# Other steps for the value pages of the paged attention in a hybrid decoder layer

## What is computed

```python
k_past = cache_k[l, page_table].reshape(db, past, N_HEADS, HEAD_DIM)
v_past = cache_v[l, page_table].reshape(db, past, N_HEADS, HEAD_DIM)
...
s = einsum('bqhd,bkhd->bhqk', q, k) * HEAD_DIM ** -0.5 + c_q - c_k
p = softmax(s)
return einsum('bhqk,bkhd->bqhd', p, v)
```

## Time and profile before

| | us |
|---|---|
| median of three runs | 2797.38 |
| lowest and highest run | 2797.11, 2801.74 |
| profiled execution | 2798.29 |
| its span, first to last instruction | 2796.3 |
| TensorE busy in the span | 2617.2 |
| VectorE busy | 1425.7 |
| ScalarE busy | 735.1 |

### The profile page before, as it was taken

How to read it: one execution, slowest core, us unless ns; L and a number is a source line. 1 busy time by engine, 2 the same in 40 slices (tenths; PEclk the granted TensorE clock), 3 DMA queues, 4 the chain that set the end, 5 groups by cost and what they waited for, 6 DMA issues and landing times.

```text
span 2796.3 us, 50751 instructions
## 1 busy us (share of the span) xinstructions
PE 2617.2 (94%) x19729; PEld 2342.8 (84%) x19729; DVE 1425.7 (51%) x5631; ACT 735.1 (26%) x1029; POOL 160.9 (6%) x326
## 2 busy tenths in 40 slices
PE   6788789999988799889999999999999999999998
PEld 3676667777776356569999999999999999999998
DVE  5698768767867622244434343434343434343433
ACT  5222123333332311132222222222222222222221
POOL 0100111111111122100000000000000000000000
PEclk8888889999989799979999999999999999999999
DMA  8778999999999897652222222222222222222221
GB/s 297 242 243 299 335 334 364 360 359 359 335 328 363 323 314 265 218 186 84 93 96 91 91 91 91 91 91 91 91 91 91 91 91 91 91 91 91 91 91 65
DMA packets 272292, 524.55 MB, mean 188 GB/s; under 512 B 16148, under 2 KB 181693, under 8 KB 270740
## 3 DMA queue, kind: packets, MB, share of 16 engines
q1 hardware_dynamic: 218717, 365.71, 38.0%
q0 software_dynamic: 39760, 142.46, 13.8%
q10 hardware_dynamic: 13575, 13.14, 1.4%
HBM read 501.84 MB, written 17.76 MB: 186 GB/s over the span
## 4 chain that ended last, share of the span: by engine, by line
PE 70%; DMA 13%; DVE 11%; issue 3%; SPq 2%; ACT 1%; POOL 0%; DVEq 0%; POOLq 0%; ACTq 0%
PE ps L749 69%; DMA t_r<-in_cache_k 9%; DVE t_r L1857 8%; DMA t_r<-in_cache_v 2%; DMA t_wraw<-in_w_in 1%; SPq L630 1%; PE ps L752 1%; DVE t_stg L1742 0%; DVE t_wlr L1686 0%; DVE t_S L1857 0%; DVE t_auxL L1686 0%; DVE t_work L1686 0%; DVE t_xl L1686 0%; SPq L683 0%; ACT t_wh L1271 0%
## 5 line engine op out<-in xcount | busy, mean ns | idle before, releaser
L749 PE MATMUL ps<-t_xh,t_wh 128*128 128x260 f32 (+1 forms) x4352 | 1080.3, 299 | 33.4 <-DVE t_wlr L1686 19.6
L749 PE MATMUL ps<-t_xl,t_wh 128*128 128x260 f32 (+1 forms) x4352 | 1053.1, 294 | 0.0
L749 PEld LDWEIGHTS ps<-t_xh,t_wh 128*128 128x128 f32 x4352 | 745.8, 193 | 166.7 <-issue 119.2
L1686 DVE TENSOR_TENSOR t_wl<-t_wraw,t_wh 128x1024 fp32r<-128x1024 f32 x296 | 362.3, 1225 | 843.7 <-ACT t_wh L1271 843.7
L1271 ACT ACTIVATE t_wh<-t_wraw 128x1024 fp32r<-128x1024 f32 x376 | 398.5, 1060 | 1479.9 <-PE ps L749 1369.8
L749 PEld LDWEIGHTS ps<-t_xl,t_wh 128*128 128x128 f32 x4352 | 744.7, 193 | 10.7 <-issue 1.4
L749 PE MATMUL ps<-t_xh,t_wl 128*128 128x260 f32 (+1 forms) x3072 | 677.1, 294 | 0.0
L1857 DVE CUSTOM_DVE_ANT_0 t_r<-t_r,t_work 128x128 f32<-128x128 f32 x2048 | 455.4, 286 | 175.3 <-DMA t_r<-in_cache_k 159.0
L749 PEld LDWEIGHTS ps<-t_xh,t_wl 128*128 128x128 f32 x3072 | 487.5, 189 | 11.8
L749 PE MATMUL ps<-t_xh,t_wlr 128*128 128x260 f32 x1280 | 376.1, 294 | 0.0
L749 PE MATMUL ps<-t_hh,t_wh 128*128 128x260 f32 x1408 | 282.8, 282 | 3.4 <-issue 3.4
(11 more groups left out here) (305 smaller groups left out, 1243.0 us busy)
## 6 DMA issues: line engine op xcount, KB each, us to landing
t_r<-in_cache_k SPq DMA_DIRECT2D x256, 512.0 KB, 6.7
t_r<-in_cache_v POOLq DMA_DIRECT2D x256, 512.0 KB, 7.0
t_wraw<-in_w_up SPq DMA_DIRECT2D x44, 2048.0 KB, 8.0
t_wraw<-in_w_down SPq DMA_DIRECT2D x22, 2048.0 KB, 7.8
t_wraw<-in_w_in SPq DMA_DIRECT2D x21, 2048.0 KB, 16.2
t_wraw<-in_w_o SPq DMA_DIRECT2D x11, 2048.0 KB, 14.0
scr_x<-t_r POOLq DMA_DIRECT2D x1, 4160.0 KB, 20.0
t_work<-in_x_prompt SPq DMA_DIRECT2D x4, 1024.0 KB, 6.6
```

Source lines behind the costliest of these rows:

```text
L749: return pe.matmul(out, lhsT, rhs, start=start, stop=stop)
L1686: return dve.tensor_tensor(out, in0, in1, op)
```

## The change

One line of `page_slots` gives other rates for the value pages. During the input projection a step takes two pages, and four in every eighth step (7, 15, 23, ...) where it was every fourth. In steps 80 to 83 it takes two where it took four. From step 84 on every step takes four, where every third took two.

```diff
         while done < PAGES:
-            rate = (4 if at % 4 == 3 else 2) if at < CHUNKS else 4 if at < OUT0 or at % 3 else 2
+            rate = (4 if at % 8 == 7 else 2) if at < CHUNKS else 2 if at < OUT0 else 4
             take = min(rate, PAGES - done)
             values[at] = [r * PAGES + done + i for i in range(take)]
             done += take
```

## The result

The changed kernel takes 2805.6 us in the median, the kernel before 2799.3 on the same chips: 1.0022 of before, with an interval of 1.0013 to 1.0031. It is 6.4 us slower, where 2.1 us faster had been forecast. The profiled execution has a span of 2803.7 us, against 2796.3 before. One execution of 13982 us, of the run that thins both bytes and products, is left out of that run's median.

A forecast was written before the change was run, and what follows sets the result against it. Projection bound mostly by the loop of key page landing, VectorE scoring and buffer reload; output steps by TensorE. -14.8 - 2.5 - 4.5 + 11.9 + 1.8 + 6 = -2.1 us: 2796.2 against the profiled run, 2795.3 beside the median; range 2781 to 2809.

The forecast's parts named there:

- Output steps: Steps 86 to 110: 11.9 us more for pairs, 1.8 for an end of a sequence, 6 for stalls.
- The pairs: Output steps: 11 more pairs of value pages at 1.08 us of TensorE each, 11.9 us slower, nothing covering it.
- 18, so 6 more than now: Output steps: TensorE's stalls for value pages rise from 12.2 us to 18; bounds of the increase 0 and 20.
- Rival B: Output steps become bound by landings and lose 30 to 34 us; kernel 8 to 12 slower, 2807; chance 0.12.
- Projection: Steps 17 to 78: eight dropped pairs win 14.8 us (bounds 0 and 22.7), moved sequence ends 2.5; about 636 us.
- the price of a pair: Projection: a dropped pair wins 2.1 us where the chain runs over key pages and VectorE, 1.08 where over TensorE.
- The step-30 term: Projection: TensorE's 7.70 us wait before its first pair at step 30 goes, winning 2.5 us, between 0 and 7.7.
- the sign that the prediction had named against itself: Projection: TensorE's wait before a sequence's first pair, at step 30, reappears in another step with a like size.
- Middle: Steps 79 to 85: TensorE's waits for value pages go, VectorE is late next; 4.5 us won, bounds 0 and 5.5.
- Tail: Behind step 110: sample softmax one step later costs nothing, covered by TensorE's output chunks; without cover up to 6.9 us.
- A: Projection held by DMA alone: 22.7 us won there, -15.5 for the kernel, so 2782; chance 0.33.
- C: Projection doesn't follow DMA load; VectorE's 488 us and order set the pace; only some 5 us won, 2807; chance 0.14.

## Why the prediction was wrong, point by point

*Output steps: the step that failed.* The forecast's sum there was 19.7 us, and 30.5 came: 10.8 more, against 3.9 more than forecast that the stages ahead won, and 2.3 that came from the steps before 17, which no edit touches. The pairs were right: TensorE's count rises from 1089 matmuls to 1177, that is 11 pairs of eight; the fourth end of a sequence, priced at 1.8, falls into step 111, where nothing more than 0.3 us came. The mis-sized term is "18, so 6 more than now" for landings: the row that it was counted from went from 12.2 to 26.5 us, 14.3 more (inside the bound of 20). Of the 18.6 us beside the pairs, the six output weight loads make about 9 (the windows with small loads on either schedule), so this mechanism was near its size. The rest came from three places that the forecast had not priced: the stores and the feed-forward load (4.6 us in steps 93 and 110, shown by moving them); the residual rows in steps 87 and 89 (the chain's landings of 9.2 us; two pages in these steps won 3.5 us beside the moved pairs); and a granted clock of 0.98 in place of 1.00 over 242 us. It is short of full in three places, steps 87, 89 and 104:

```profile
948.79:964.06 15.27, 12.68 (x66) 7.64 (x62) 3.17 (x4) 2.65 (x5) 3.16 (x6) 0.89 1.01 364
971.95:986.12 14.17, 11.71 (x62) 6.47 (x58) 2.18 (x2) 2.64 (x3) 2.11 (x4) 0.88 0.70 253
1118.77:1128.11 9.34, 9.34 (x42) 5.63 (x42) 0.53 (x2) 0.81 (x1) 1.06 (x2) 0.83 0.58 198
```

The first two hold the longest waits; the third holds none. Counted as the missing share of each step's time, that is an estimated 5 us of slower work, against 1 before. These parts overlap and were found on different runs, so they are not a sum. Rival B had the sign and the size (30 to 34) and was given 0.12: it counted stalls from weight loads only, and would have needed both pairs to fall short at each. That isn't what happened: at each load one pair fell short, with under 0.5 us left for the step behind, and other transfers did the rest. That its time, 2807, lies within 2 us of the measured one is luck in part, since the stages ahead won 25.7 us where it counted 21.8.

The forecast said that nothing urgent stands behind POOL's waits "except two stores of small rows". It asked what the pages hold up, and not what holds the pages up: these stores stand ahead of step 93's pages. And of the feed-forward load in step 110 it said nothing, though the change moves the last pages from step 109 onto it.

*Projection: right sum, wrong reason.* 636 us was forecast and 633.9 came, and VectorE waited for key pages

```profile
DVE t_r L1857 <- DMA t_r<-in_cache_k: 128.4, 26, 14.8
```

against 138.2 us (about 120 was forecast). But the price of a pair, 2.1 us for its landing, is refuted: without the bytes, without the products and without both, the whole kernel's time can't be told from before. All ten profiled kernels with the new rate lie between 631 and 638 us, and all ten with the old one, these cuts and the moved ends included, between 647 and 664. What the traces do show is a coupling in both directions. SP holds the key pages behind a weight load until TensorE has freed its buffer (28.1 us in 6 waits before, 21.5 in 5 after), and TensorE waits with its small products until VectorE has read the bank that they share (5.9 us in step 69 before, 7.6 in step 33 after). That a lead of one engine alone is lost at the next such place fits the run with the ends one step later, but is argued, not shown. Which property of the new rate keeps the lead is still open; that two waits for buffers vanish with each pair wasn't tried by itself. The step-30 term (-2.5) is in the same sum: that wait did go, and others of like size appeared (7.6 us in step 33, 6.2 in step 74). They are waits of small products for VectorE and none stands before the first pair of a sequence, so they are not the sign that the prediction had named against itself.

*Middle: right in its mechanism.* -4.5 was forecast, with 5.5 as the bound, and -6.6 came. TensorE's waits for pages fell from 10.3 us to 6.0 (4.53, 1.00 and 0.46), VectorE is late next, and TensorE stands before the product of the sample rows:

```profile
905.73 3.12 PE L749 MATMUL ps<-t_r,t_work 128*8 128x512 f32 x8 [4.53 <-DMA t_r<-in_cache_v]
...
937.28 1.90 PE L749 MATMUL ps<-t_wraw,t_work 128*8 128x256 f32 x16 [9.32 <-issue]
```

The forecast had all the waits for pages go; 6.0 us of them stayed.

*Tail: right.* Nothing was forecast, 0.3 us came, covered as said; one step later cost 4 to 9 us in the three runs with the last page in step 111 (the 9 with two pairs of pages in that step).

*The answer to A and C.* A (the projection gives all, 22.7 for bytes) is refuted by the thinned pages. C has two parts. That the projection doesn't follow the DMA load agrees with the same run; that VectorE's own work alone sets the pace does not hold, since VectorE is as busy as before (489.13 us) in a stage 19 us shorter.

## What to carry to other kernels

When a stage gets more transfers into a small ring, list everything that shares the queue or the engines with each refill: not the regular loads alone, but one-time stores in the issuing engine's program and the first load of the next stage, which a step with spare time may have hidden. Before pricing a dropped transfer by its share of the DMA engines, ask which engine waits for which in the stage; where two engines wait for each other, taking work from one may win nothing, as it did here. And test the reason for a gain too: here its sum was right and its reason was not.

## What the runs showed that was not expected

Eight stores of a few rows cost POOL 4.0 us of issue time and held the next page's issue back by 6 us in all. Spreading 2 MB loads raised the median landing of a page from 4.6 to 5.8 us while TensorE's idle time before value pages fell from 15.7 to 7.2: the few long landings cost more than the median shows. And a long wait of TensorE can cost more than itself. In the run without steps of two pages, the granted clock was at full speed until TensorE stood for 10.35 us, and at half, the lower of its two levels (1.2 in place of 2.4 GHz), for 5.5 us after it, in which a chunk's matmul takes 0.63 us in place of 0.40:

```profile
1000.00:1008.00 8.00, 8.00 (x38) 4.56 (x32) 0.00 (x0) 0.00 (x0) 2.11 (x4) 1.00 1.09 348
1018.54:1024.00 5.46, 5.46 (x17) 3.02 (x18) 0.15 (x1) 0.00 (x0) 1.06 (x2) 0.50 0.30 82
```
